# Carried state products of the grid stage: another PSUM bank, earlier steps, additions on GpSimd

## The reference, cut to what matters

```
seg  = cum[i] - cum[j];  decay = exp(where(lower, seg, -inf))
m    = (C B^T) * decay * dt                       # one 128-token tile pair per head
y    = m @ x  +  (C @ h_in) * exp(cum)            # the second term: carried state
y    = (y_f + flip(y_b) + d_skip * x) * silu(z);  y = rms_norm(y)
```

## Time and profile before

| | us |
|---|---|
| median of three runs | 1003.0 (1001.48 to 1005.24) |
| profiled execution, its own time | 1004.7 |
| its span | 1002.9 |
| PE busy | 966.2 |
| DVE busy | 682.4 |
| ACT busy | 517.8 |
| GpSimd busy | 53.0 |

### The profile page before, as it was taken

One profiled execution on the slowest core, in us unless ns is written; L12 is line 12 of the kernel. 1 busy time (PEld: TensorE's weight loads), 2 busy tenths in 40 slices (PEclk: granted clock), 3 DMA queues, 4 the chain that ended last, 5 costly groups with the idle time before them and its releaser, 6 DMA issues. The chain is left out here.

```text
span 1002.9 us, 14868 instructions
## 1 busy us (share of the span) xinstructions
PE 966.2 (96%) x5844; PEld 828.4 (83%) x5844; DVE 682.4 (68%) x948; ACT 517.8 (52%) x715; POOL 53.0 (5%) x71
## 2 busy tenths in 40 slices
PE   7989999999999999999999999999988989999997
PEld 4468898998977877899988887889865789999996
DVE  2576658999755666647777674467565687777775
ACT  2465565445446665554544554454566454444443
POOL 0310000000001110000000000000001000000000
PEclk9999999999999999999999999999997999999999
DMA  9132566768656732678888562232210536555541
GB/s 364 64 104 97 213 258 215 287 216 287 252 200 192 239 126 90 218 286 295 311 313 312 193 252 63 106 126 85 85 43 7 194 123 227 182 180 182 182 170 42
DMA packets 28944, 185.05 MB, mean 185 GB/s; under 512 B 3680, under 2 KB 4384, under 8 KB 9312
## 3 DMA queue, kind: packets, MB, share of 16 engines
q1 hardware_dynamic: 23472, 155.54, 43.1%
q0 software_dynamic: 4416, 28.31, 7.6%
q10 hardware_dynamic: 1008, 0.55, 0.2%
HBM read 181.76 MB, written 2.62 MB: 184 GB/s over the span
## 5 line engine op out<-in xcount | busy, mean ns | idle before, releaser
L2020 DVE TENSOR_TENSOR split<-raw,split 128x2048 fp32r<-128x2048 f32 x122 | 279.6, 2292 | 179.0 <-ACT split L1460 177.4
L1460 ACT ACTIVATE split<-raw 128x2048 fp32r<-128x2048 f32 x121 | 231.5, 1913 | 234.0 <-PE bank L727 204.7
L725 PE MATMUL bank<-acts,split 128*128 128x256 f32 (+1 forms) x960 | 278.2, 290 | 2.8 <-DVE acts L2060 1.4
L727 PE MATMUL bank<-acts,split 128*128 128x256 f32 (+1 forms) x960 | 276.7, 288 | 0.0
L726 PE MATMUL bank<-acts,split 128*128 128x256 f32 (+1 forms) x960 | 276.7, 288 | 0.0
L725 PE MATMUL bank<-split,acts 128*128 128x512 f32 (+1 forms) x544 | 211.6, 389 | 3.0 <-DVE acts L2702 1.6
L726 PE MATMUL bank<-split,acts 128*128 128x512 f32 (+1 forms) x544 | 208.8, 384 | 0.0
L727 PE MATMUL bank<-split,acts 128*128 128x512 f32 (+1 forms) x544 | 208.6, 383 | 0.0
L725 PEld LDWEIGHTS bank<-acts,split 128*128 128x128 f32 x960 | 183.7, 191 | 10.5 <-DVE split L2020 3.9
L726 PEld LDWEIGHTS bank<-acts,split 128*128 128x128 f32 x960 | 183.8, 191 | 3.4
L727 PEld LDWEIGHTS bank<-acts,split 128*128 128x128 f32 x960 | 183.7, 191 | 1.9
(11 more groups left out here) (251 smaller groups left out, 1023.6 us busy)
## 6 DMA issues: line engine op xcount, KB each, us to landing
raw<-w_mlp SPq DMA_DIRECT2D x64, 1024.0 KB, 4.8
raw<-w_glu SPq DMA_DIRECT2D x22, 1024.0 KB, 4.7
bias<-w_ada POOLq DMA_DIRECT2D x14, 1024.0 KB, 6.9
raw<-w_qkv SPq DMA_DIRECT2D x12, 1024.0 KB, 5.2
arena<-w_glu_down SPq DMA_DIRECT2D x22, 512.0 KB, 3.3
work<-w_ada POOLq DMA_DIRECT2D x10, 1024.0 KB, 5.7
raw<-w_mla_o SPq DMA_DIRECT2D x4, 1024.0 KB, 5.1
raw<-w_moba_o SPq DMA_DIRECT2D x4, 1024.0 KB, 4.7
```

The source lines that it names most:

```text
L725: pe.matmul(out_, a[0], b[0], start=first, stop=False)
L727: return pe.matmul(out_, a[1], b[0], start=False, stop=last)
L1460: return act.activation(out_, in_, ACT.Copy)
L2020: v.tensor_tensor(split[:, c % 2, 1, 0:n], raw[:, c % 2, 0:n], split[:, c % 2, 0, 0:n].bitcast(F32), ALU.subtract).then_inc(lo_ready, 1)
```

## The change

F no longer uses the segment bank: all four products go to `y_banks[0]`, which the first Y takes over in step 4, and have semaphores of their own (`carry_ready`, `carry_free`). The segment bank is left to G alone. F0 and F1 keep their places. F2 moves from step 6 to step 3, between S3 and Z3; F3 moves from step 9 to the end of step 3, behind O0. DVE multiplies F0 in step 2, F1 and F2 in step 3, and F3 in step 4 after `pair_scaled(0)`, into two alternating buffers. GpSimd does the four additions to `yrow`: the first ahead of mask addition 1, the other three ahead of mask addition 2. Y0 waits until DVE has read F3. `pair_rows` and `inverse_rows` get one buffer each in place of two, to make room.

PE's order after, from step 3: `P3 S3 F2 Z3 R0 O0 F3 | P4 G2 Y0 | P5 S4 G3 Y1 | P6 | P7 S5 G4 Y2 R1 O1 | P8 G5 Y3 | P9 S6 | P10 G6 Y4 | P11 S7 G7 Y5 R2 O2 | P12`.

```diff
-CARRIED = (2, 3, 7, 10)
+CARRIED = {2: (0,), 3: (1, 2)}
...
+        if i == 3:
+            steps.append(("F", 2))
         if i < 4:
             steps.append(("Z", i))
...
+        if i in (1, 2):
+            steps.append(("F", i - 1))
         if i in WEIGHTED:
             steps.append(("R", WEIGHTED.index(i)))
             steps.append(("O", WEIGHTED.index(i)))
+        if i == 3:
+            steps.append(("F", 3))
...
+            def carried_rows_in(n):
+
+                pool.wait_ge(carry_free, n + 1)
+                if n:
+                    pool.wait_ge(carried_added, n)
+                pool.tensor_tensor(yrow[:, n // 2, :], yrow[:, n // 2, :], carried[:, n % 2, :], ALU.add)\
+                    .then_inc(carried_added, 1)
+
             for h in range(H):
+                for n in {1: (0,), 2: (1, 2, 3)}.get(h, ()):
+                    carried_rows_in(n)
                 pool.wait_ge(w_mat, h + 1)
...
                 elif kind == "F":
                     t, d = i // 2, i % 2
-                    segment_start(kind, i)
+                    if i == 0:
+                        gemm_gone(pe, ku + 5)
+                    else:
+                        pe.wait_ge(carry_free, i)
                     for g in range(2):
-                        ins = pe.matmul(seg_bank[:, g * 256:(g + 1) * 256], CT[:, g, t * P:(t + 1) * P],
+                        ins = pe.matmul(y_banks[0][:, g * 256:(g + 1) * 256], CT[:, g, t * P:(t + 1) * P],
                                         h0T[:, d, g * 256:(g + 1) * 256], start=True, stop=True)
-                    ins.then_inc(seg_ready, 1)
+                    ins.then_inc(carry_ready, 1)
                 else:
                     if i == 0:
-                        for u in (ku + 5, GU["z"] + 1):
-                            gemm_gone(pe, u)
+                        gemm_gone(pe, GU["z"] + 1)
+                        pe.wait_ge(carry_free, 4)
...
             def carried_rows(n):
 
                 t, d = n // 2, n % 2
-                tm = arena[:, 1024:1536]
+                tm = carried[:, n % 2, :]
+                if n >= 2:
+                    v.wait_ge(carried_added, n - 1)
                 settle()
                 v.wait_ge(ecum_ready, 1)
-                segment_out(v, "F", n)
+                v.wait_ge(carry_ready, n + 1)
                 c = 320 + 16 * d + 8 * t
-                v.tensor_tensor(heads(tm), heads(seg_bank[:, :]), spread(stat[:, c:c + 8], 1, 64), ALU.mult)\
-                    .then_inc(seg_free, 1)
-                v.wait_ge(seg_free, SEGMENTS.index(("F", n)) + 1)
-                settle()
-                step(v.tensor_tensor(yrow[:, t, :], yrow[:, t, :], tm, ALU.add))
+                v.tensor_tensor(heads(tm), heads(y_banks[0][:, :]), spread(stat[:, c:c + 8], 1, 64), ALU.mult)\
+                    .then_inc(carry_free, 1)
...
             def gated_rows(t):
 
                 v.wait_ge(y_ready, t + 1)
+                v.wait_ge(carried_added, 2 * t + 2)
...
-                if i in CARRIED:
-                    carried_rows(CARRIED.index(i))
+                if i < 4:
+                    for n in CARRIED.get(i, ()):
+                        carried_rows(n)
...
                 if i in (4, 8, 12):
                     pair_scaled(i // 4 - 1)
+                if i == 4:
+                    carried_rows(3)
```

More of the change, by code:

```diff
@@ L183 @@
 DECAY = (0, 1, 5, 6, 8, 9, 11, 12)
-CARRIED = (2, 3, 7, 10)
-SEGMENTS = [("G", 0), ("G", 1), ("F", 0), ("F", 1), ("G", 2), ("G", 3), ("F", 2), ("G", 4), ("G", 5), ("F", 3), ("G", 6), ("G", 7)]
-SEGMENT_STEP = {**{("G", h): DECAY[h] - 1 for h in range(1, H)}, **{("F", n): CARRIED[n] - 1 for n in range(4)}}
+CARRIED = {2: (0,), 3: (1, 2)}
+SEGMENT_STEP = {DECAY[h] - 1: h for h in range(1, H)}
 MIXED = (4, 5, 7, 8, 10, 11, 13, 14)
@@ L198, in grid_order @@
             steps.append(("S", (i + 3) // 2))
+        if i == 3:
+            steps.append(("F", 2))
         if i < 4:
             steps.append(("Z", i))
-        else:
-            steps.extend(x for x in SEGMENTS if x[0] == "G" and SEGMENT_STEP.get(x) == i)
+        elif i in SEGMENT_STEP:
+            steps.append(("G", SEGMENT_STEP[i]))
         if i in MIXED:
             steps.append(("Y", MIXED.index(i)))
-        steps.extend(x for x in SEGMENTS if (x[0] == "F" or i < 4) and SEGMENT_STEP.get(x) == i)
+        if i < 4 and i in SEGMENT_STEP:
+            steps.append(("G", SEGMENT_STEP[i]))
+        if i in (1, 2):
+            steps.append(("F", i - 1))
         if i in WEIGHTED:
@@ L341, in program @@
         h0T = view(work, 5120, 2, NA)
-        pair_rows, inverse_rows = view(arena, 13824, 2, T), view(arena, 1536, 2, T)
+        pair_rows, inverse_rows = arena[:, 13824:14080], arena[:, 14080:14336]
+        carried = view(arena, 1024, 2, 2 * T)
         gact = view(arena, 1024, 2, T)
@@ L425, in program @@
         seg_ready, seg_free = sem("segment_ready"), sem("segment_free")
+        carry_ready, carry_free = sem("carried_products_ready"), sem("carried_products_free")
         y_ready, y_free = sem("state_rows_ready"), sem("state_rows_free")
@@ L428, in program @@
         w_summed = sem("mask_diagonals_summed")
+        carried_added = sem("carried_rows_added")
         z_act = sem("gate_rows_activated")
@@ L485, in program, with segment_out @@
         parts = ((0, 256, 0, 0), (256, 384, 128, 1), (384, 512, 256, 0), (512, 768, 256, 1))
-        def segment_out(eng, kind, i):
-            eng.wait_ge(seg_ready, SEGMENTS.index((kind, i)) + 1)
+        def segment_out(eng, h):
+            eng.wait_ge(seg_ready, h + 1)
         def released(eng, c, i=None, per=0):
@@ L1254, in _, with segment_start @@
             rows_units(kc + 1, ku + 3, KD, 256, 256, both[:2])
[L1256 to L1260, removed]
+            def segment_start(h):
+                if h:
+                    pe.wait_ge(seg_free, h)
                 else:
@@ L1320, in grid_work @@
                 elif kind == "G":
-                    segment_start(kind, i)
+                    segment_start(i)
                     if i == 0:
@@ L1387, in _ @@
             pe.wait_ge(y_free, 1)
-            pe.wait_ge(seg_free, len(SEGMENTS))
+            pe.wait_ge(seg_free, H)
             out_chunk(0, 0, (0,))
@@ L1841, in pair_out @@
                 act.wait_ge(pair_free, p + 1)
-                copy(acts[:, 0, 0, p * T:(p + 1) * T], pair_rows[:, p % 2, :]).then_inc(out_hi, 1)
+                copy(acts[:, 0, 0, p * T:(p + 1) * T], pair_rows).then_inc(out_hi, 1)
             def gate_rows_out(t):
@@ L1864, in decay @@
             def decay(h):
-                segment_out(act, "G", h)
+                segment_out(act, h)
                 if h >= 2:
@@ L1873, in decay @@
                 ins.then_inc(seg_free, 1)
-                act.wait_ge(seg_free, SEGMENTS.index(("G", h)) + 1)
+                act.wait_ge(seg_free, h + 1)
                 act.activation(E[h % 2], E[h % 2], ACT.Exp, scale=-1.0).then_inc(seg_exp, 1)
@@ L2694, in pair_scaled @@
                 small_out(v, u)
-                v.tensor_copy(inverse_rows[:, p % 2, :], sbank(u)[:, 0:T]).then_inc(small_free[u % 4], 1)
+                v.tensor_copy(inverse_rows, sbank(u)[:, 0:T]).then_inc(small_free[u % 4], 1)
                 small_gone(v, u)
                 v.wait_ge(pair_ready, p + 1)
-                v.tensor_tensor(pair_rows[:, p % 2, :], pair_bank[:, 0:T], inverse_rows[:, p % 2, :], ALU.mult).then_inc(pair_free, 1)
+                v.tensor_tensor(pair_rows, pair_bank[:, 0:T], inverse_rows, ALU.mult).then_inc(pair_free, 1)
             def pair_lo(p):
                 v.wait_ge(out_hi, 2 * H + p + 1)
-                v.tensor_tensor(acts[:, 0, 1, p * T:(p + 1) * T], pair_rows[:, p % 2, :],
+                v.tensor_tensor(acts[:, 0, 1, p * T:(p + 1) * T], pair_rows,
                                 acts[:, 0, 0, p * T:(p + 1) * T].bitcast(F32), ALU.subtract)\
```

## The result

The changed kernel takes 1007.55 us in the median of 9 runs (1004.78 to 1008.10), the kernel before 1003.0 in 9 runs beside it: ratio 1.0035, 95% interval 1.0023 to 1.0046. The change makes the kernel slower by a third of a per cent. The profiled execution went from 1004.7 to 1007.55, its span from 1002.9 to 1005.8.

A forecast was written before the change was run, and what follows sets the result against it. The grid stage was taken as bound by PE, outside holes where ACT and DVE set the pace. +2.0 (F2, F3, DVE's queue), -1.75 (F3's old place) and +0.4 (GpSimd meeting) made +0.7: 1003.0 to 1003.7 us, range 998.7 to 1008.8.

The forecast's parts named there:

- the rival with the clock: PE's clock falls in step 7, in a 3.0 us hole ahead of S5: +4.9 in all, 1007.9; chance 0.33.
- F2's old place is worth 0: Step 6: removing F2 saves nothing, since S5 waits for ACT's exponential of step 9.
- F3's old place is worth 1.78: Step 9: without F3 head 5's matrix waits only for ACT's decay exponential, opening 1.78 us of slack.
- F2 and F3 in step 3, and the wait in DVE's queue, +2.0: Steps 3 and 4: both products lengthen PE's path, F3's multiplication holds step 7's logits; S4 starts 2.0 us later.
- GpSimd's meeting with the matrix of head 1, +0.4: GpSimd's first addition shares DVE's inputs, DVE loses 1.3, S3 comes 0.4 us later, between 0 and +0.6.
- Net on the chain +0.7: Sum in the grid stage: +2.0 for steps 3 and 4, -1.75 for F3's old place, +0.4 for the meeting.
- the 4.2 worked out from the longest fall: Price of a fall from S5 to P8: S7 to P12 at the lower level 8.80, S5 to P8 4.64.
- the prediction's own sign of being wrong: Stated sign of a wrong forecast: a clock of 0.50 in another place than ahead of S7.
- The fall at S7: Forecast keeps the clock's fall in the 1.8 us hole ahead of S7; rival, clock holds, 999.5, chance 0.15.

The follow-up runs named there:

- e4: Kernel before with F2, its multiplication and its addition left out: 1006.05 us, ratio 1.0025.
- e2: Changed kernel with spare PE products, results thrown away, 3 ahead of S5 and 2 ahead of S7: 1001.91 us, ratio 0.9982.
- e8: Kernel before with F3, its multiplication and its addition left out: 1000.80 us, ratio 0.9971.
- e10: Kernel before with F2 behind P6 and F3 behind P7, in the head pairs' bank, plus two spare products ahead of S7: 998.94 us, ratio 0.9952.
- e5: Kernel before with one spare PE product between P6 and F2 and two ahead of S7: 1000.44 us, ratio 0.9976.
- e6: Changed kernel with the four additions back on DVE, each behind its multiplication: 1007.19 us, ratio 1.0036.
- e1: Changed kernel with three spare PE products, results thrown away, between P7 and S5: 1003.82 us, ratio 1.0003.
- e11: Changed kernel measured again as it is, 12 runs: 1007.25 us, ratio 1.0031.
- e3: Kernel before with two spare PE products between P11 and S7: 1001.16 us, ratio 0.9974.
- e7: Kernel before with the four additions on GpSimd, no product moved, one buffer each for `pair_rows` and `inverse_rows`: 1004.35 us, ratio 1.0002.
- e9: Kernel before with F2 behind P6 and F3 behind P7, both in the head pairs' bank: 1001.19 us, ratio 0.9973.

## Why the prediction was right, and where it was not

The time lies in the stated range and within the 0.5%, but the forecast of 1003.7 was 3.9 too low. The range holds the result because it was drawn to hold the rival with the clock, not because the sum was right. (Its upper end should read 1008.7, 1007.9 + 0.8.) By its steps:

- **F2's old place is worth 0:** right. S4 to S5 is 6.73 to 6.75 in before, after, and e4 without F2 (shown).
- **F3's old place is worth 1.78:** right. S6 to S7 is 1.74 shorter in after, e2, e8 and e10 (shown).
- **F2 and F3 in step 3, and the wait in DVE's queue, +2.0:** 2.22 measured. F2, between S3 and the dense Z, made O0 0.87 later (its end moved by 1.25, S3's start by 0.38), as taken. F3, behind O0, takes 1.08 on the chain and not 0.86, and its multiplication starts 1.20 behind its start where I had taken 0.99 (0.86 + 0.13):

```profile
735.42 1.73 PE bank L1326 x16
737.15 1.08 PE bank L1359 x4
...
738.35 0.69 DVE arena L2754
```

- **GpSimd's meeting with the matrix of head 1, +0.4:** 0.15 measured at S3, though DVE lost 1.04 of the expected 1.3. That explains most of the difference. GpSimd's 128 x 512 takes 1.27 to 1.47; 1.48 was the upper bound, and the prediction's estimate of 1.1 was too low. The Trainium skill, "SBUF — State Buffer", section "SBUF: two separate sides", calls the shared pair an exclusive lock. These rows agree in kind: 1.04 and 1.02 lost on DVE beside additions of 1.47 and 1.45, which started 0.16 and 0.17 behind the first of the four instructions on DVE; the loss of the whole 1.48 that I had drawn from its rule was too much.
- **Net on the chain +0.7:** S2 to S7 at full clock is 39.60 in e2 against 38.93 in before and 38.96 in e5: +0.64 to +0.67. Right.
- **The step that failed is the clock in step 7.** I had the mechanism as the rival (hole of 3.0 us, 1007.9) and gave it 0.33, below the forecast. The hole was 3.18, and the clock fell in it in both profiled executions of the changed kernel, and in e4 and e6 1.0 and 0.7 us behind its end. That it fell in about two of three single runs is an estimate from their times (15 of 21 runs above 1006); only the profiled runs show it. The fall also met the prediction's own sign of being wrong, a clock of 0.50 in another place than ahead of S7. e1 takes the fall away and lands at 1003.82, on the forecast; e4 makes it without the change. Its price was 3.17 in the first profile, since the clock came back in the middle of O1, 3.21 and 3.24 in e4 and e6, and 4.37 in e11, against the 4.2 worked out from the longest fall. So that the rival's 1007.9 lies next to the measured 1007.55 is in part luck: its +4.9 would be a ratio of 1.0049, above the interval. I had set against it that holes of 2.05 us in 3.6 did nothing before. In e3, whose PE program is the same up to there, the clock fell just behind the first of these holes (S4 to S5 and S5 to S6 together 1.0 longer): one profile in which a hole does nothing is no proof that it is harmless.
- **The fall at S7** stayed, as forecast; in the first profile it came about 1.5 us behind S7's start, so that S7 itself still took 1.13. It is not certain either: in e6, behind the same hole of 1.81, the clock held without filler and S7 to T is 19.77.

What stays open: what exactly PE must do in a stretch to keep its clock, and whether e8 gained more than its chain. Delaying F3's multiplication behind the logits of step 7 was not tried.

## What to carry to other kernels

Before moving work out of a hole on PE, ask what fills the hole afterwards: work whose place costs nothing can be what keeps the clock, and its removal can cost more than it weighs. Look for a free place that is idle anyway (here a bank unused for two steps) rather than one on the dense path. And an instruction moved earlier on an in-order engine holds everything queued behind it: count from when its input is ready, not from its own length.

## What the runs showed of the hardware

- PE's granted clock is not the same from run to run of one program: 0.993 to 0.999 for the kernel before, with 1000.1 to 1007.1 us, in all its runs beside the experiments. A profile shows one draw; here a change of 3 us was told from nothing over 9 to 12 runs.
- One and the same hole can pass or not. Behind the 1.50 us of step 6 the clock fell in e3 (742.7) and not in before, e7 and e8. Ahead of S7, with a hole of 1.80 to 1.84 us, it fell in the hole in five profiles (before at 758.1, e1, e7, e9, e11), 0.9 to 1.6 us behind it in three (after, e4, e8), and not there in e6. With 1.7 us of spare products in that hole it held at S7 in all four profiles (e2, e3, e5, e10). e2 and e10 fell once later, at 769.6 and 766.4, in the tail of the stage, where S7 to T is 0.40 and 0.28 longer than in e5.
- Once down, the clock stayed at 1.2 GHz for 3.4 us (e3, e8), 6.8 (after, both falls; e1, e7, e9) or 10.2 (before, e11's first), with PE busy for over nine tenths of the time; in the changed kernel's first fall it was busy for 6.78 of 6.90 us.
- A mask addition of 128 x 256 on GpSimd takes 0.73 and an addition of 128 x 512 1.27 where DVE does not meet it (after, 728.35 and 730.06); an estimate from these two is 0.19 fixed and 0.54 for 256 columns. Beside four two-input instructions of DVE the larger one takes 1.44 to 1.47 and DVE's four 2.41 to 2.44 in place of 1.40 (after, e7).
